# An even mixer with unturned bias rows, gates computed feature-major, diagonal products for the head pairs, and a closing norm on three engines

## What the reference computes

```
h <- LN(a*h + 1/2*g_0*SwiGLU_a(mod_0(h)))
h <- LN(a*h + g_1*W_out[mixers(mod_1(h) W_in)])
h <- LN(a*h + 1/2*g_2*SwiGLU_b(mod_2(h)))
```

## Time and profile before

| | us |
|---|---|
| median of three runs (2026.27 to 2027.99) | 2026.64 |
| the profiled execution, its own time | 2024.13 |
| its span, first to last instruction | 2022.4 |
| busy in the span: PE / DVE / ACT / POOL | 1917.7 / 1263.6 / 644.7 / 290.5 |
| mean granted TensorE clock, as a share of full | 0.967 |

### The profile page before, as it was taken

One profiled execution on the slowest core, in us unless ns is written; L12 is line 12 of the kernel. 1 busy time (PEld: TensorE's weight loads), 2 busy tenths in 40 slices (PEclk: granted clock), 3 DMA queues, 4 the chain that ended last, 5 costly groups with the idle time before them and its releaser, 6 DMA issues.

```text
span 2022.4 us, 24268 instructions
## 1 busy us (share of the span) xinstructions
PE 1917.7 (95%) x9246; PEld 1523.2 (75%) x9246; DVE 1263.6 (62%) x2215; ACT 644.7 (32%) x1093; POOL 290.5 (14%) x318
## 2 busy tenths in 40 slices
PE   5999999999998789899999989999999899989997
PEld 5888878885553454788887878888778867879997
DVE  7677776742883572777778357774777535464454
ACT  2322242323343431422224233222423232334442
POOL 0000001150000002400000231000044535130003
PEclk7999999998998899899999999999999999989999
DMA  9354535313360001355444233544134544214542
GB/s 361 126 204 170 206 142 162 135 54 125 115 231 9 1 1 42 121 201 198 177 161 183 95 150 121 203 179 155 73 117 190 222 180 177 84 42 167 186 164 108
DMA packets 43959, 290.12 MB, mean 143 GB/s; under 512 B 13916, under 2 KB 19676, under 8 KB 27232
## 3 DMA queue, kind: packets, MB, share of 16 engines
q1 hardware_dynamic: 34336, 270.08, 35.6%
q10 hardware_dynamic: 9536, 18.88, 2.5%
HBM read 272.16 MB, written 16.78 MB: 143 GB/s over the span
## 4 chain that ended last, share of the span: by engine, by line
PE 84%; DVE 9%; ACT 3%; DMA 2%; issue 1%; POOL 1%; SPq 0%; ACTq 0%; POOLq 0%; DVEq 0%
PE bank L613 13%; PE bank L618 13%; PE bank L615 13%; PE bank L670 7%; PE bank L679 6%; PE bank L676 6%; PE bank L807 4%; PE bank L804 3%; PE bank L791 3%; PE bank L1001 2%; PE bank L744 2%; PE bank L734 1%; PE bank L998 1%; DVE L L1729 1%; PE bank L956 1%
## 5 line engine op out<-in xcount | busy, mean ns | idle before, releaser
L1729 DVE CUSTOM_DVE_ANT_0 L<-slot 128x1024 f32<-128x1024 f32 x272 | 337.7, 1241 | 72.1 <-DMA slot<-in_ada_dram 64.9
L1185 ACT ACTIVATE w_hi<-slot 128x1024 fp32r<-128x1024 f32 x176 | 186.2, 1060 | 571.4 <-PE bank L618 559.2
L1786 DVE TENSOR_TENSOR w_lo<-slot,w_hi 128x1024 fp32r<-128x1024 f32 x176 | 216.9, 1235 | 217.8 <-ACT w_hi L1185 212.0
L613 PE MATMUL bank<-m_hi,w_hi 128*128 128x512 f32 (+1 forms) x1344 | 296.6, 363 | 3.2 <-ACT w_hi L1185 3.2
L615 PE MATMUL bank<-m_lo,w_hi 128*128 128x512 f32 (+1 forms) x1344 | 296.1, 362 | 0.0
L618 PE MATMUL bank<-m_hi,w_lo 128*128 128x512 f32 (+1 forms) x1344 | 296.1, 362 | 0.0
L613 PEld LDWEIGHTS bank<-m_hi,w_hi 128*128 128x128 f32 x1344 | 232.3, 189 | 43.1 <-ACT w_hi L1185 4.0
L615 PEld LDWEIGHTS bank<-m_lo,w_hi 128*128 128x128 f32 x1344 | 232.6, 189 | 39.3
L618 PEld LDWEIGHTS bank<-m_hi,w_lo 128*128 128x128 f32 x1344 | 232.6, 189 | 39.3
L1945 DVE TENSOR_TENSOR down_lo<-slot,down_hi 128x1408 fp32r<-128x1408 f32 x64 | 108.6, 1709 | 128.5 <-ACT down_hi L1235 128.3
L676 PE MATMUL bank<-g_lo,down_hi 128*128 128x512 f32 (+1 forms) x770 | 156.5, 351 | 0.1
(11 more groups left out here) (348 smaller groups left out, 2616.8 us busy)
## 6 DMA issues: line engine op xcount, KB each, us to landing
slot<-in_gateup_dram SPq DMA_DIRECT2D x44, 2048.0 KB, 7.5
slot<-in_ada_dram SPq DMA_DIRECT2D x34, 2048.0 KB, 7.5
slot<-in_down_dram SPq DMA_DIRECT2D x32, 1408.0 KB, 5.9
slot<-in_ev_in_dram SPq DMA_DIRECT2D x4, 2048.0 KB, 9.7
slot<-in_od_in_dram SPq DMA_DIRECT2D x4, 2048.0 KB, 10.1
R<-s_ops SPq DMA_DIRECT2D x16, 512.0 KB, 6.8
s_tables<-slot ACTq DMA_DIRECT2D x8, 768.0 KB, 3.3
R<-s_tables SPq DMA_DIRECT2D x8, 768.0 KB, 7.4
```

Of the source, the lines that this page charges most:

```text
L613: nc.tensor.matmul(bank[j][:, c0:T], w_hi[:, off, c, :], m_hi[:, c, c0:T], start=(c == 0), stop=False)
L1185: nc.scalar.activation(w_hi[:, off, :, :].rearrange("p a b -> p (a b)"), slots[b][:, (2 * (f % 2) + off) * D:(2 * (f % 2) + off + 1) * D], ...
L1729: ins = nc.vector.tensor_tensor_reduce(out=junk, in0=slots[k][:, t * D:(t + 1) * D], in1=csilu[s_], scale=1.0, scalar=0.0, op0=ALU.mult, o ...
L1786: nc.vector.tensor_tensor(w_lo[b][:, t, :, :].rearrange("p a b -> p (a b)"), slots[b][:, t * D:(t + 1) * D], w_hi[:, off, :, :].bitcast(F3 ...
```

## The change

1. The bias keeps its reversed rows. The latent q columns are stored in reverse within each tile of 128 tokens (so that score rows are reversed as well), the mask is turned once, by one 64-column product ahead of ffn0 and one DVE copy in it, DVE adds the mask from slot 2 before the first convolution, and the attention output is reversed back in the DVE copy that exists already. The eight `turn_bias` products go.
2. The 16 gate columns are spread by POOL to 128 (each kind at a multiple of 32), and eight products with 512 moving columns give all gates feature-major. ACT reads the four kinds at once, ahead of n = 6. The 16 transposes and one copy go.
3. In the head pairs DVE gives only the reciprocals. ACT writes them on a diagonal (the identity times the reciprocal), and PE multiplies the unscaled probabilities with this diagonal instead of transposing scaled ones. `turned_probs` of a pair moves behind the next pair's diagonals.
4. Closing norm: DVE subtracts the mean of tile 7; ACT applies gain and bias to six tiles and POOL to two (4 and 6); SP issues the output transfers.

```diff
+        diag = view(R, 5632, 4, P)
-        gates_tok = view(L, 6 * T, TT, 16)
+        gate_w = slots[1][:, KT * 16:KT * 16 + KT * P].rearrange("p (c a b) -> p c a b", a=4, b=32)
+        ACT_OUT, POOL_OUT = (0, 1, 2, 3, 5, 7), (4, 6)
...
-                            sp.wait_ge(sem("na_bias_turned"), 8)
+                            sp.wait_ge(sem("na_bias_masked"), 8)
...
+            for d in range(KT):
+                if d in POOL_OUT:
+                    sp.wait_ge(sem("h_ready"), before("h_ready", "ffn3") + POOL_OUT.index(d) + 1)
+                else:
+                    sp.wait_ge(sem("out_ready"), ACT_OUT.index(d) + 1)
+                sp.dma_start(out[:, d, :], h[:, d, CTX:T]).then_inc(sem("out_written"), 16)
...
             early_modulation()
+            pe.wait_ge(sem("even_params_in"), 16 * 7)
+            nc.tensor.matmul(banks[7][:, 0:GRID_W], flip[:, :], na_mask[:, :], start=True, stop=True).then_inc(sem("na_mask_turned"), 1)
...
-                for n in range(4):
-                    turn_bias(n)
...
-                        for n in range(4, 8):
-                            turn_bias(n)
...
-                    for t in range(TT):
-                        for c in range(KT):
-                            last = nc.tensor.matmul(banks[4][:, 16 * t:16 * t + 16], m[:, c, t * P:(t + 1) * P], gw[:, c, :],
-                                                    start=(c == 0), stop=(c == KT - 1))
+                    pe.wait_ge(sem("gates_spread"), 2)
+                    for c in range(KT):
+                        last = nc.tensor.matmul(banks[4][:, :], gate_w[:, c, :, :].rearrange("p a b -> p (a b)"), m[:, c, :], start=(c == 0), stop=(c == KT - 1))
...
-                        pe.wait_ge(sem("na_probs_ready"), u + 1)
+                        pe.wait_ge(sem("na_diag_ready"), u + 1)
                         if p:
                             pe.wait_ge(sem("na_pT_ready"), u - 1)
                         for kt in range(tiles):
-                            last = nc.tensor.transpose(banks[2 + u % 2][:, kt * P:(kt + 1) * P], probs[u % 4][:, kt * P:(kt + 1) * P], ident[:, :])
+                            last = nc.tensor.matmul(banks[2 + u % 2][:, kt * P:(kt + 1) * P], probs[u % 4][:, kt * P:(kt + 1) * P], diag[:, u % 4, :],
+                                                    start=True, stop=True)
...
+                    if n < 12:
+                        turned = lambda v: v[:, CTX:T].rearrange("p (a n) -> p a n", n=P)
+                        nc.scalar.activation(turned(dst)[:, :, ::-1], turned(src), ACT.Copy, scale=NA_DIM ** -0.5)
+                        dst, src = dst[:, 0:CTX], src[:, 0:CTX]
...
                     if p + 1 < NA_PAIRS:
                         exps(p + 1)
-                    turned_probs(p)
+                    act.wait_ge(sem("na_rec_ready"), p + 1)
+                    for u in (2 * p, 2 * p + 1):
+                        nc.scalar.activation(diag[:, u % 4, :], ident[:, :], ACT.Copy, scale=col[:, 8 + u % 4:9 + u % 4]).then_inc(sem("na_diag_ready"), 1)
+                    if p:
+                        turned_probs(p - 1)
+                turned_probs(NA_PAIRS - 1)
...
+            for d in ACT_OUT:
+                act.wait_ge(sem("z"), KT * halves("ffn3", 1) + d + 1)
+                nc.scalar.activation(h[:, d, CTX:T], h[:, d, CTX:T], ACT.Identity, bias=lnb[:, 5, d:d + 1],
+                                     scale=lng[:, 5, d:d + 1]).then_inc(sem("out_ready"), 1)
...
-                    link(nc.vector.reciprocal(col[:, 8 + a:10 + a], col[:, 4 + a:6 + a]))
-                    for u in (2 * p, 2 * p + 1):
-                        keys = CTX if UNITS[u][1] == 0 else T
-                        nc.vector.tensor_scalar(probs[u % 4][:, 0:keys], probs[u % 4][:, 0:keys], col[:, 8 + u % 4:9 + u % 4], None,
-                                                ALU.mult).then_inc(sem("na_probs_ready"), 1)
+                    nc.vector.reciprocal(col[:, 8 + a:10 + a], col[:, 4 + a:6 + a]).then_inc(sem("na_rec_ready"), 1)
...
+                pool.wait_ge(full[1], 16 * (uses_before("even")[1] + 1))
+                nc.gpsimd.memset(gate_w.rearrange("p c a b -> p (c a b)"), 0.0).then_inc(sem("gates_spread"), 1)
+                pool.wait_ge(sem("gates_spread"), 1)
+                nc.gpsimd.tensor_copy(gate_w[:, :, :, 0:4], slots[1][:, 0:KT * 16].rearrange("p (c a b) -> p c a b", a=4, b=4)).then_inc(sem("gates_spread"), 1)
```

More of the change, by code:

```diff
@@ L699, in ffn @@
                 norm_stats(name, 1)
[L701 to L706, removed]
             def norm_stats(name, s_):
@@ L1417, in even @@
                         act.wait_ge(used[1], slot_done[1])
-                        nc.scalar.activation(gates_tok.rearrange("p a b -> p (a b)"), banks[4][:, 0:TT * 16], ACT.Copy).then_inc(sem("even_gates_read"), 1)
+                        for kind in range(4):
+                            nc.scalar.activation(rows[:, kind, :], banks[4][32 * kind:32 * kind + HEADS, :], ACT.Identity,
+                                                 bias=gate_b[:, kind:kind + 1]).then_inc(sem("even_rows_ready"), 1)
                     projected("even", n, 3)
@@ L1423, in even @@
                     nc.scalar.activation(xc[:, hd, :], xc[:, hd, :], ACT.Silu)
-                for kind in range(4):
-                    act.wait_ge(sem("even_rows_done"), kind + 1)
-                    nc.scalar.activation(rows[:, kind, :], banks[4 + kind][0:HEADS, :], ACT.Identity, bias=gate_b[:, kind:kind + 1]).then_inc(sem("even_rows_ready"), 1)
                 act.wait_ge(sem("even_rows_step"), 1)
@@ L1599, in _ @@
                     odd()
-            for d in range(KT):
-                act.wait_ge(sem("h_ready"), before("h_ready", "ffn3") + d + 1)
-                act.dma_start(out[:, d, :], h[:, d, CTX:T]).then_inc(sem("out_written"), 16)
+            for d in ACT_OUT:
+                act.wait_ge(sem("z"), KT * halves("ffn3", 1) + d + 1)
+                nc.scalar.activation(h[:, d, CTX:T], h[:, d, CTX:T], ACT.Identity, bias=lnb[:, 5, d:d + 1],
+                                     scale=lng[:, 5, d:d + 1]).then_inc(sem("out_ready"), 1)
         @block.vector
@@ L1770, in _, with mask_bias @@
             early_modulation(ada_early[1])
[L1772 to L1778, removed]
+            def mask_bias():
+                dve.wait_ge(sem("na_bias_in"), 16 * ROWS * ROWS)
+                cols = lambda v: v.rearrange("p a (r c) -> p (a r) c", c=GRID_W)
+                for n in range(8):
+                    part = slice(2 * (n % 4), 2 * (n % 4) + 2)
+                    nc.vector.tensor_tensor(cols(na_bias[:, n // 4, part, :]), cols(bias_flipped[:, n // 4, part, :]),
                                             na_mask[:, :].unsqueeze(1).to_broadcast([P, 2 * ROWS, GRID_W]), ALU.add).then_inc(sem("na_bias_masked"), 1)
@@ L1877, in norm @@
                 statistics(first)
+                if name == "ffn3":
+                    link(nc.vector.tensor_tensor(h[:, KT - 1, CTX:T], h[:, KT - 1, CTX:T], mean[:, CTX:T], ALU.subtract))
                 inverse(first)
@@ L1962, in ffn @@
                             rest(0, s_, d)
+                    dve.wait_ge(sem("na_mask_turned"), 1)
+                    link(nc.vector.tensor_copy(na_mask[:, :], banks[7][:, 0:GRID_W]))
                 n_ada = ADA_IN[name][1]
@@ L2290, in attention_out @@
                 dve.wait_ge(sem("na_out_done"), 2 * group + 2)
-                nc.vector.tensor_copy(y[:, hp, a:b], banks[4 + group % 2][:, 0:CTX]).then_inc(sem("even_y0"), 1)
+                dst, src = (v.rearrange("p (a n) -> p a n", n=P) for v in (y[:, hp, a:b], banks[4 + group % 2][:, 0:CTX]))
+                nc.vector.tensor_copy(dst, src if st == 0 else src[:, :, ::-1]).then_inc(sem("even_y0"), 1)
             nc.vector.memset(ones_w[:, :], 1.0).then_inc(sem("mean_w_ready"), 1)
@@ L2420, in centre @@
                     pool.wait_ge(sem("stat_read"), 3 * halves(name, s_) + 1)
-                    for d in range(KT):
+                    for d in range(KT - 1 if name == "ffn3" else KT):
                         if d == KT - 1:
@@ L2430, in gains @@
                     pool.wait_ge(sem("m_lo_ready"), before_lo(s, 1) + KT)
-                for d in range(KT):
+                for d in range(KT) if n + 1 < 6 else POOL_OUT:
                     if n + 1 < 6:
```

17 lines of the change are left out of this document (3 added, 14 removed).

## The result

| | before | after |
|---|---|---|
| median, us (range, runs of the same chip) | 2026.27 (2025.27 to 2027.99, 5) | 2036.16 (2033.52 to 2038.36, 5) |
| ratio after / before, 95% interval | | 1.0048 [1.0037, 1.0058] |
| the profiled execution / its span | 2024.13 / 2022.4 | 2035.15 / 2033.4 |
| busy PE / DVE / ACT / POOL | 1917.7 / 1263.6 / 644.7 / 290.5 | 1916.3 / 1252.1 / 656.0 / 289.8 |
| mean granted clock | 0.967 | 0.968 |

A forecast was written before the change was run, and what follows sets the result against it. The prediction took PE to bound the kernel (84% of the chain), with a loop of waits in the head pairs. Joins -13.8, closing norm -3.4 and head pairs +29.6 gave +12.4: 2039 on the median, forecast as 2038, range 2023 to 2052.

The forecast's parts named there:

- The step from 2039 down to 2038: Whole kernel: lowered to 2038 because terms no row shows directly (diagonals, copies) are more often overlapped than not.
- Joins, 13.81 less: Even stage's projections on PE: bias products 6.86, transposes 1.75, gates 3.69 and slow clock 1.51 saved.
- the slow clock behind them: Projection tiles behind the narrow gate products: full clock without those products, 1.51 us less.
- Closing norm, 3.4 less, bounds 2.8 and 4: End of kernel: last write issued at 2016.6 to 2016.8 in place of 2020.1.
- Head pairs, 29.6 more: Even stage's head pairs: longer loop of waits; three fours 22.6 more, first two pairs 4.5, end 2.5.
- The 0.35 for `weigh` and scores: Each four of head pairs: at the lower clock they outlast the loop's other arm, adding 0.35 us.
- The end: Last of the head pairs: two latent products at 3.6 and 2.7 against 1.97 and 1.86, 2.5 us more.
- the long gap that the prediction named: Before the first latent pair of a four: PE idle 4.2 us, so its product begins at the lower clock, 1.80 more.
- The value of a four without that, 21.05: Head pairs: one four of the new loop at the upper clock takes 21.05 us.
- The rival in which the upper clock holds: Head pairs: three fours take 63.2, pairs +16.8 in all, kernel 2026, no slower; chance 0.18.
- The cheap product: Head pairs: a diagonal product costs what the transpose did; a four is 18.4, kernel 2017 with clock up; chance 0.08.
- The clock never recovers: Head pairs: clock stays low, a four goes to about 27, kernel +26 at 2053; chance 0.14.

The follow-up runs named there:

- old_pairs: The changed kernel with the head pairs of before (DVE scales, PE transposes, ACT copies at once), joins and closing norm kept; 2011.14 us.
- narrow_gates: `old_pairs` with its gate products undone as well: 16-column products turned back by 16 transposes, no weights spread; 2017.24 us.
- filler: The changed kernel with 12 unread products on PE in the gap ahead of the first latent pair of each four; 2033.65 us.
- rec_first: The changed kernel with DVE's reciprocals of pair p before maxima of p+1, and ACT's diagonals of p, exponentials of p+1, copies of p in that order; 1999.03 us.
- scale_first: `old_pairs` with DVE's reciprocal and scalings of pair p ahead of the maxima of pair p+1; 2004.80 us.
- copy_back: The changed kernel with ACT's bank copies of pair p straight behind the diagonals of pair p; 2028.87 us.

## Why the prediction was right, step by step

The forecast of 2038 stands 1.8 above the measured 2036.16. The sum on the profiled execution was +12.4, and the spans show +11.0. The closeness is in part luck: the closing norm won back 1.1 less than priced, and the head pairs cost 2.7 less, and the two errors go against each other in the sum. The step from 2039 down to 2038 had no row behind it. As a difference of medians the forecast was +11.4 and the result is +9.9.

- *Joins, 13.81 less*: measured 13.83. `old_pairs` and `narrow_gates` show the terms: gates and transposes back cost 3.76 + 1.75, the slow clock behind them 1.46 (priced 1.51). None of the waits that could have taken their place appeared. POOL began the spreading at 437.46 and not at 433.29, because its gains took 11.33 and not 7.39; the slack hid that.
- *Closing norm, 3.4 less, bounds 2.8 and 4*: measured 2.3, outside the bounds. The arithmetic engines came out as priced, counted from the copy of the mean. The last multiplication ended at 8.2; the prediction had 8.4, where its own rows (2011.74 + 4.76 = 2016.50) give 8.7. ACT's last gain ended at 8.8 (priced 8.8 to 9.0). The subtraction given to DVE took 0.94 and moved the start of the reciprocal from 2.15 to 2.57; the multiplications won back 0.93 (3.83 in place of 4.76). What failed is the end of the list, which was put at nothing. POOL's gain of tile 4 took 1.17 and not 0.68, and was done at 8.5. SP issues in order, so tiles 4, 5, 6 and 7 left one after the other from there, about 0.46 apart, and the last was issued at 9.8 in place of 8.8 to 9.0. The 0.68 was the mean of two prices, 1.08 beside DVE's multiplications and 0.54 behind them. The Trainium skill (SBUF — State Buffer, shared port pair) says that a DVE instruction with two SBUF inputs and a GpSimd instruction that reads SBUF exclude each other. The trace agrees: the subtraction took 0.94 against 0.43 for others, the multiplications 0.86 against 0.33, POOL's gains 1.08 to 1.17 against 0.54. The prediction used the rule for a gain of perhaps 0.3 alone; it gave 0.9, and the same rule has the price of tile 4's gain in it.
- *Head pairs, 29.6 more*: measured 26.9. The loop was named right, link by link, and most of its terms were right: two diagonals 0.58 (priced 0.66, bounds 0.34 to 1.02), latent product 2.04 and 3.77 (2.00 and 3.80), context 1.14 to 1.18 (1.10). Fours took 23.0, 23.0 and 22.8, priced 23.2, together 21.8 more (22.6); the first two pairs cost 3.8 more (4.5) and the end 1.3 (2.5). The 0.35 for `weigh` and scores doesn't show: behind the slow product the chain goes straight to DVE's maxima. The end was mis-sized: the last product had the upper clock, 2.00 against 2.7, and the `weigh` between the two products took 1.27, where before it took 1.91.
- *The clock*: it was down at the first latent product of each four, as forecast, but not always by the long gap that the prediction named: once it fell ahead of that gap. The value of a four without that, 21.05, is close to what `filler` gave, 21.3 to 21.65. The rival in which the upper clock holds was refuted.
- *The cheap product*: refuted. A record costs 0.13 us, in a product (2.04 / 16) as in a transpose (1.04 / 8), and a product has two.
- *The clock never recovers*: refuted; PEclk in the fours was 0.80 to 0.87.
- Not in the account: ffn0 +0.3, the mLSTM and output projection +0.8, the middle -0.9. They cancel; no run took them apart, and the joins' influence on the loads of the middle stays open.

What the prediction did not see is that the loss belongs to the order of two lists and not to the diagonal products. It priced the order that was written, and that was right for the time; `rec_first`, with the same instructions, is 37 us faster.

## What to carry to other kernels

When scaling moves from one engine to another, write out the loop of waits again with each engine's list, and place what the next product needs (reciprocal, diagonal) ahead of work for a later pair: the order that cost 5.5 us with the scaling on DVE (`old_pairs` against `scale_first`) cost 26.1 with it on ACT (`copy_back` against `rec_first`). Look at the lists of both engines; here DVE's alone gained nothing (99.0), and both together with the copies gained 36 of 96 us. Count the clock in PE's idle gaps too: the dense four of `rec_first` kept the upper level throughout, and filling the gaps of the changed kernel was worth 6.0 in its stretch. A mean over instructions that overlap another engine's work in part (0.68 for POOL's gain) is not the price of one of them at the end of the chain.

## What the runs showed of the hardware

- A 128x128 ACT copy with one pointer takes 0.29 us in the chain, 0.39 by its own record.
- DVE instructions with two SBUF inputs on 256 columns took 0.94 (a subtraction) and 0.86 (two multiplications) while POOL was subtracting, and 0.33 each afterwards. POOL was slowed as well (its last two subtractions took 0.9 each). The mean of the eight multiplications (0.48) hides this.
- POOL's gain on 256 columns took 1.08 to 1.17 beside DVE's multiplications and 0.54 behind them; the mean of eight is 0.68. DVE's last multiplications weren't slowed by it (0.33 each).
- Twelve unread products in PE's gap (2.94 us of PE at the upper clock, up to 4.37 where it was low) saved 1.45 us of each four: the clock was up when the next product came.
